# High and low weight parts for 24 units of layers 0 and 1, made at fixed places of ScalarE's and VectorE's programs

## The reference

```
# layer 0
h = rmsnorm(x); u_val, u_gate, z_a, q_b, k_b, v_b, z_b = split(h @ e_w_in)
y_a = conformer_conv(u_val, u_gate) * silu(z_a)
y_b = moba_attention(norm(q_b), norm(k_b), v_b) * silu(z_b)
x = x + concat(y_a, y_b) @ w_out[0]
# layer 1
h = rmsnorm(x); q_c, kc, vc, ks, vs, kw, vw, g_c, z_c, q_d, k_d, v_d, z_d = split(h @ o_w_in)
y_c = nsa_attention(...) * silu(z_c);  y_d = banded_attention(...) * silu(z_d)
x = x + concat(y_c, y_d) @ w_out[1]
# layer 2: modulated norm, retention and dilated attention, gates, then a squared-relu MLP
mod = silu(c) @ w_ada + b_ada          # 12 column groups, ad0 to ad11, spread over layers 0 and 1
x = x + g1 * token_mixer(modulate(rms_norm(x), sh1, sc1))
x = x + g2 * mlp(modulate(rms_norm(x), sh2, sc2));  out = rms_norm(x)
```

## Time and profile before

| | us |
|---|---|
| median of 3 runs | 1032.57 (1030.12 to 1032.97) |
| the profiled execution's own time | 1030.22 |
| its span | 1028.4 |
| PE busy | 957.8 (93%) |
| DVE, ACT, POOL busy | 363.5, 408.1, 446.0 |

### The profile page before, as it was taken

One profiled execution on the slowest core, in us unless ns is written; L12 is line 12 of the kernel. 1 busy time (PEld: TensorE's weight loads), 2 busy tenths in 40 slices (PEclk: granted clock), 3 DMA queues, 4 the chain that ended last, 5 costly groups with the idle time before them and its releaser, 6 DMA issues.

```text
span 1028.4 us, 15967 instructions
## 1 busy us (share of the span) xinstructions
PE 957.8 (93%) x6896; PEld 874.2 (85%) x6896; DVE 363.5 (35%) x734; ACT 408.1 (40%) x588; POOL 446.0 (43%) x101
## 2 busy tenths in 40 slices
PE   4999889999898798999999998999999979999996
PEld 4887677788676377999999998999999979999996
DVE  4677521320556626640111113222115643341002
ACT  3111541013576423234343444667533545553330
POOL 0000000000000031787766665766787767886780
PEclk9999899999899999999999998999999989999998
DMA  9632245858524363565534443444544625453531
GB/s 353 257 123 82 83 175 205 329 176 316 196 83 164 124 246 126 175 242 183 185 131 158 158 150 111 160 161 152 177 164 164 238 95 200 168 199 130 204 121 41
DMA packets 27470, 177.51 MB, mean 173 GB/s; under 512 B 2904, under 2 KB 5476, under 8 KB 6920
## 3 DMA queue, kind: packets, MB, share of 16 engines
q1 hardware_dynamic: 25960, 174.28, 46.9%
q10 hardware_dynamic: 1440, 2.20, 0.7%
HBM read 174.88 MB, written 3.43 MB: 173 GB/s over the span
## 4 chain that ended last, share of the span: by engine, by line
PE 84%; DVE 10%; ACT 3%; issue 1%; DMA 1%; POOL 0%; DVEq 0%; ACTq 0%
PE proj L571 18%; PE proj L596 14%; PE proj L597 14%; PE proj L598 14%; PE proj L628 3%; PE proj L630 3%; PE proj L629 3%; PE proj L780 3%; PE proj L617 2%; PE transposed L702 2%; PE proj L810 2%; PE mixed L731 1%; PE scores L690 1%; DVE parts L1561 1%; PE scores L677 1%
## 5 line engine op out<-in xcount | busy, mean ns | idle before, releaser
L521 POOL TENSOR_TENSOR w_lo<-raw,w_hi 128x2048 fp32r<-128x2048 f32 x71 | 329.0, 4639 | 269.7 <-ACT w_hi L1050 269.6
L596 PE MATMUL proj<-parts,w_hi 128*128 128x256 f32 x768 | 222.2, 289 | 6.5 <-DVE parts L1383 4.2
L597 PE MATMUL proj<-parts,w_lo 128*128 128x256 f32 x800 | 227.5, 284 | 0.0
L598 PE MATMUL proj<-parts,w_hi 128*128 128x256 f32 x768 | 218.3, 284 | 0.0
L1050 ACT ACTIVATE w_hi<-raw 128x2048 fp32r<-128x2048 f32 x71 | 135.5, 1909 | 99.4 <-PE proj L598 63.8
L596 PEld LDWEIGHTS proj<-parts,w_hi 128*128 128x128 f32 x768 | 148.1, 193 | 8.1 <-issue 5.2
L597 PEld LDWEIGHTS proj<-parts,w_lo 128*128 128x128 f32 x800 | 154.2, 193 | 0.8 <-issue 0.7
L598 PEld LDWEIGHTS proj<-parts,w_hi 128*128 128x128 f32 x768 | 148.0, 193 | 0.0
L525 POOL MEMSET probT<- 128x512 f32 x1 | 0.5, 525 | 247.8 <-PE proj L897 247.8
L571 PE MATMUL proj<-h,raw 128*128 128x256 f32 x320 | 76.5, 403 | 3.0 <-DVE h L1391 3.0
L571 PEld LDWEIGHTS proj<-h,raw 128*128 128x128 f32 x320 | 64.7, 204 | 14.2 <-issue 4.5
(11 more groups left out here) (273 smaller groups left out, 1940.5 us busy)
## 6 DMA issues: line engine op xcount, KB each, us to landing
raw<-in_weights SPq DMA_DIRECT2D x113, 1024.0 KB, 4.9
arena<-in_weights SPq DMA_DIRECT2D x36, 1024.0 KB, 5.0
probT<-in_weights SPq DMA_DIRECT2D x8, 1024.0 KB, 5.7
dil_lines<-dil_line SPq DMA_DIRECT2D x1, 2304.0 KB, 12.1
dil_bias<-dil_lines SPq DMA_DIRECT2D x1, 1536.0 KB, 9.6
xT<-in_x SPq DMA_DIRECT2D x2, 512.0 KB, 5.6
arena<-in_alibi SPq DMA_DIRECT2D x1, 1024.0 KB, 20.6
arena<-in_swa SPq DMA_DIRECT2D x1, 1024.0 KB, 7.3
```

The lines of the kernel that those rows point to most:

```text
L521: nc.gpsimd.tensor_tensor(lo_slots[RAW_AT[n]][:, 0:kt * w], raw_slots[RAW_AT[n]][:, 0:kt * w], hi_slots[HI_AT[m]][:, 0:kt * w].bitcast(F32 ...
L596: nc.tensor.matmul(dst, whi, h, start=first, stop=False)
L597: nc.tensor.matmul(dst, wlo, h, start=False, stop=False)
L598: last = nc.tensor.matmul(dst, whi, lo[:, k, :], start=False, stop=stop)
```

## The change

24 units of layers 0 and 1 (all that are not uv, ug, bq, bk, bv, kcvc, the ad units or the hidden layers' ck and cv) join the list `SPLIT`, and are multiplied as high and low parts, three products for one float32 matmul. For the first 23 of them ACT makes the high copy (`high`) and DVE, not POOL, the subtraction (`low`), each called at a place written into its program; the 24th, wo1_3, stays with POOL, which now begins its list with it. The activations are split too: h of layers 0 and 1 (`high_parts` without a shift), and the gated outputs yT0 and yT1. The raw slots and the order of the loads change: slots 6 to 8 hold parts too, slot 8 lies under h of layer 0 (`h0`) and is not used before bv1 is done, ad units from ad6 on use slots 0 to 3, and wo1_0 to wo1_2 are loaded ahead of ad7. The diff, cut to its core:

```diff
@@ tables @@
+    "/ zd1.1", "/ E:zd1 ad6", "/ modA", "/ ad7", "/ ad8", "Y:c / ad9", "/", "/ ad11")]
-SPLIT = WEIGHTS[WEIGHT_AT["rq0"]:]
+WHOLE = ("uv0", "ug0", "uv1", "ug1", "bq0", "bq1", "bk0", "bk1", "bv0", "bv1", "kcvc")
+SPLIT = [u for u in WEIGHTS if u not in WHOLE and u[:2] not in ("ad", "ck", "cv")]
+BY_POOL = SPLIT_AT["wo1_3"]
+HIGH_B, LOW_B = {1: "za1", 2: "wo0_0", 3: "wo0_1"}, {2: "za1", 3: "wo0_0"}
+HIGH_CD = {0: "zc1", 2: "zd0", 3: "zd1", 5: "wo1_0", 7: "wo1_1", 9: "wo1_2"}
+LOW_CD = {1: "zc1", 3: "zd0", 4: "zd1", 6: "wo1_0", 8: "wo1_1", 10: "wo1_2"}
@@ PE, weight(u) @@
-                pe.wait_ge(lo_ready, m + 1)
+                if m < BY_POOL:
+                    pe.wait_ge(sem("lo_early"), m + 1)
+                else:
+                    pe.wait_ge(lo_ready, m - BY_POOL + 1)
@@ PE, layer 1 @@
             project("kcvc", fresh=1)
+            pe.wait_ge(h_ready, 2 * KD)
             project("kskw")
-            plain_tokens("vsvw", 2 * P)
+            tokens("vsvw", 0, 2 * P)
...
-            plain_tokens("vdgt", P + 24)
+            tokens("vdgt", 0, P + 24)
@@ ACT @@
+            def high(u):
+                n, m = WEIGHT_AT[u], SPLIT_AT[u]
+                kt, w = unit_shape(u)
+                if HI_BEFORE[m] is not None:
+                    act.wait_ge(proj_ready, LAST_READ[SPLIT[HI_BEFORE[m]]] + 1)
+                act.wait_ge(raw_in[RAW_AT[n]], raw_target(n))
+                nc.scalar.activation(hi_slots[HI_AT[m]][:, 0:kt * w], raw_slots[RAW_AT[n]][:, 0:kt * w], ACT.Copy).then_inc(hi_ready, 1)
@@ ACT, output_squares: between the squares of one group and of the next @@
+                    if i < len(also):
+                        high(also[i])
-            output_squares(0, "x1")
+            output_squares(0, "x1", ("wo0_3", "kskw", "vsvw"))
+            high_parts("x1")
+            high("qc0")
@@ ACT, layer 1 @@
             root("kskw")
+            high("vdgt")
             head_squares("qc0", fl(qcT[:, 0:2]))
+            high("qd0")
             head_squares("qc1", fl(qcT[:, 2:4]))
+            high("zc0")
             root("qc0")
...
             hidden_copy(0, "hidk")
+            high("qd1")
             head_squares("qd0", fl(qdT[:, 0:2]))
+            high("kd")
             hidden_silu(0, "hTk", "c_k_b1")
@@ DVE @@
+            def low(u):
+                dve.wait_ge(hi_ready, m + 1)
+                V.tensor_tensor(lo_slots[RAW_AT[n]][:, 0:kt * w], raw_slots[RAW_AT[n]][:, 0:kt * w],
+                                hi_slots[HI_AT[m]][:, 0:kt * w].bitcast(F32), ALU.subtract).then_inc(sem("lo_early"), 1)
@@ DVE, layer 1 @@
             head_norm_end("kskw", "kskw", None, None)
-            for i, name in enumerate(("qc0", "qc1")):
+            low("qc1")
+            low("vdgt")
+            for name, unit in (("qc0", "qd0"), ("qc1", "zc0")):
+                low(unit)
                 variance(name)
                 head_norm_end(name, name, None, None)
+            low("qd1")
+            low("kd")
             variance("qd0")
```

More of the change, by code:

```diff
@@ L142, in raw_slots_of @@
 def raw_slots_of(n, u):
-    if u in SPLIT_AT:
+    if u[:4] == "ad10" or u[:3] == "wo1":
+        return EARLY
+    if u[:2] == "ad" and n > WEIGHT_AT["zd1"]:
+        return range(NRAW)
+    if n >= WEIGHT_AT["rq0"]:
         return range(NRAW + sum(n >= WEIGHT_AT[start] for start in RAW_MORE))
-    return EARLY if n >= WEIGHT_AT["wo1_0"] else [*range(NRAW), *EARLY]
+    return [*range(NRAW), *EARLY[:3 if n >= WEIGHT_AT["wo0_0"] else 2]]
 RAW_AT, RAW_BEFORE = take_slots(WEIGHTS, raw_slots_of)
@@ L156 @@
 LOADS.insert(LOADS.index("rq1") + 1, "wo1_3")
+for _n in range(3):
+    LOADS.remove(f"wo1_{_n}")
+    LOADS.insert(LOADS.index("ad7a"), f"wo1_{_n}")
 def loads_after():
@@ L1140, in between @@
                 if "." in name:
+                    return
+                if name[:2] == "Y:":
+                    operand_high([(hi_of(i), two(yT1, i), [(po_free, STEPS_TO["c"])]) for i in range(2)])
                     return
@@ L1187, in attention @@
                     transposed_out(u, range(1, key_tiles(u)))
+                    for made in (HIGH_B if UNITS[u][0] == "b" else HIGH_CD if UNITS[u][0] in "cd" else {}).get(i, "").split():
+                        high(made)
                     if UNITS[u][0] == "a":
@@ L1223, in _ @@
             root("bk0")
+            high("zb0")
             root("bk1")
+            high("zb1")
             copy_tokens("bv0", bv[:, :, 0:256])
+            high("za0")
             copy_tokens("bv1", bv[:, :, 256:512])
@@ L1228, in _, with output_squares @@
             attention(PART["b"], FILL_B)
+            operand_high([(hi_of(i), two(yT0, i), [(sem("y_a_ready"), i + 1)] if i < 2 else
+                           [(po_free, 2 * i - 2)]) for i in range(4)])
+            high("wo0_2")
             table(ACT.Sqrt)
-            def output_squares(layer, stream):
+            def output_squares(layer, stream, also=()):
                 for i in range(4):
@@ L1247, in _ @@
             head_squares("kskw", arena[:, L + 2048:L + 2560])
+            high("qc1")
             values = cut(ready("vsvw")[:], S)
@@ L1285, in _ @@
             attention(PART["c"] + PART["d"], FILL_CD)
+            operand_high([(hi_of(i), two(yT1, i), [(po_free, STEPS_TO["c"] + 2 * i - 2)]) for i in range(2, 4)])
             table(ACT.Sqrt)
@@ L1649, in conv_between @@
                         mixed_out(u - 1)
+                    if i in LOW_B:
+                        low(LOW_B[i])
                     if i == 0:
@@ L1675, in _ @@
             V.tensor_copy(bn[:, 1, 9:10], yT0[:, 0, 0:1]).then_inc(sem("conv_done"), 1)
+            for u in ("zb0", "zb1", "za0"):
+                low(u)
             conv_between(PART["b"])
+            parts_low(yT0)
+            low("wo0_1")
             def fold_squares(name, i):
@@ L1690, in residual @@
                     fold_squares(f"x{layer + 1}", i)
-            residual(0)
+                    if i < len(also):
+                        low(also[i])
+            residual(0, ("wo0_2", "wo0_3", "kskw"))
+            ada_out("ad2")
             stream_norm("x1", col("norm_g", 8, 8))
-            for name in ("ad2", "ad3"):
-                ada_out(name)
+            low("vsvw")
+            ada_out("ad3")
+            low("qc0")
             own.did(V.memset(blocks[:, :, :, 2 * NCMP:HROW], 0.0))
@@ L1724, in _ @@
             attention(PART["c"] + PART["d"], FILL_CD)
+            parts_low(yT1, range(2, 4))
             residual(1)
```

135 lines of the change are left out of this document (81 added, 54 removed).

## The result

The changed kernel takes **1072.37 us**, median of 4 runs (1069.89 to 1074.20); the kernel before took 1032.26 beside it (1030.12 to 1032.97, 4 runs). The ratio is 1.0391, with a 95% interval of 1.0362 to 1.0419. The profiled execution took 1073.51 with a span of 1071.7 (before 1030.22 and 1028.4), so the two spans, 43.3 apart, can be compared stage by stage.

What follows compares the result with a forecast made beforehand. PE, busy 93% of the span, was taken to bound the kernel. A gain of 20.5 us against added waits, vdgt and clock summed to +42.6 on 1032.6, so 1075 us; range 1057 to 1092, with rivals 2 to 5 1055 to 1095.

Steps and rivals of the forecast that it cites:

- The gain on PE: 18 full-width units outside the attention of layer 1, each 1.14 us shorter when split: -20.5 us.
- vdgt: Unit with 152 moving columns, taken to go no faster split than in float32, 12.7 us against 4.24: +8.5 us.
- Layer 0: Attention and output start of layer 0: PE waits 2.8 us for za1 and 3.8 at wo0_0 behind DVE's subtractions: +6.6.
- Squares of x1: End of layer 0: ACT's squares of wo0_3 stand behind vsvw's copy, which waits for its load: +7.9 us.
- qc1: Layer 1: DVE subtracts qc1 only behind the norm of kskw, so PE waits: +3.5 us.
- zc0 and qd1: Layer 1: ACT's copies wait for loads ahead of hidk's copy and qd0's squares; 6.0 and 11.1 us: +17.1 together.
- Attention of layer 1: Six copies and six subtractions delay PE's transposes by 13 us, less 3 from shorter half units: +10 us.
- Output of layer 1: wo1_3 stays with POOL, whose work meets the fold of squares, as before: net +0.5 us on top of the gain.
- Clock: Six waits of 2.8 to 8 us lower PE's granted clock behind them, 1.5 us each: +9 us.
- signs that were named: x1 sums wait over 6 us, copies wait 5 or more, vdgt 12, clock near 0.5; refuted if PE idles under 10.
- Rival 1: All new waits are covered and only PE's gain is left: 1007 to 1015 us; chance 0.05.
- Rival 5: POOL's later subtractions meet DVE's norm of x2, two collisions of 4.5 us: 1084 us; chance 0.05.

Runs made afterwards that it cites:

- e3: Changed kernel with DVE's subtractions of za1, wo0_0 and qc1 put earlier and ACT's copy of wo0_1 behind the high parts of yT0: 1065.38 us, ratio 1.0300.
- e6: The best version: e5 with ACT's high copy of zc0 behind the activation of hTk and the copy of hidv: 1017.63 us, ratio 0.9856.
- e5: Changed kernel with the moves of e1b, e2, e3 and the second reordering of layer 1's attention together: 1018.77 us, ratio 0.9862.
- e1: Changed kernel with ACT's copies and DVE's subtractions of zc0, qd1 and kd moved later in their programs: 1059.99 us, ratio 1.0258.
- e1b: e1 with the copies of qd1 and kd ahead of cmp's root, their subtractions ahead of cmp's variance: 1057.49 us, ratio 1.0238.
- e2: Changed kernel with ACT's copies of kskw and vsvw behind x1's squares and root, and DVE's subtraction of kskw later: 1062.27 us, ratio 1.0277.
- e7: e6 with ACT's squares ahead of its high copies for POOL's units in the output of layer 1: 1021.16 us, ratio 0.9895.

## Why the prediction was right, and where it was wrong

1075 was forecast and 1072.4 measured, on the mechanism that was named. By its steps:

- **The gain on PE** (-20.5): a split unit takes 5.8 us. PE's busy time in the best version is 934.7 us against 957.8, 23.1 less; 20.5, some 5 for the half units in the attention, and 1.1 back for vdgt make 24.6. The Trainium skill (FP8 and Floating Point Precision, TensorE Precision Notes) says that true FP32 makes four passes; by that the term would have been -31.1 without the half units, an estimate, and it is not seen.
- **vdgt** (+8.5): wrong. The step took the float32 row of the same shape as the nearer bound. Groups of the kernel after, 242.5 to 248.1 us:

```profile
L653 PE MATMUL proj<-w_hi,parts 128*128 128x152 f32 x16 | 4.4, 277 | 0.0
L654 PE MATMUL proj<-w_lo_e,parts 128*128 128x152 f32 x16 | 4.4, 276 | 0.0
L655 PE MATMUL proj<-w_hi,parts 128*128 128x152 f32 x16 | 4.4, 276 | 0.0
```

  The durations overlap; the 48 run from 242.61 to 248.0 at a clock of 1.00, 5.3 us against 4.24: +1.1. Neither bound held; it lies between them, nearer the low one.
- **Layer 0** (+6.6): the waits of 2.8 and 3.4 us are there. e3 gave 3.5 us of them back in this stage.
- **Squares of x1** (+7.9): the wait at the last sums is 5.7 us. kskw's copy had held the squares before, for which PE waits 1.8 us more, a wait that the forecast took for nothing. Together they are 7.5. Moving both copies gave 11.3 us in the stage (98.3 to 86.9), its clock included.
- **qc1** (+3.5): the wait is 3.5.
- **zc0 and qd1** (+17.1): waits of 5.9, 7.4 and 1.4 where 6.0 and 11.1 were forecast; with their clock the move gave 16.9 us in the stage.
- **Attention of layer 1** (+10): the stage grew by 15.0. PE's busy time in it is 3.5 us above that of the best version, with the same instructions: clock, which the forecast had as a term of its own. That leaves some 11.5 for the term.
- **Output of layer 1** (-4.6 of gain, +0.5): -2.4 measured. The step that failed is "PE waited before too": ACT's squares of wo1_1 now stand 3.4 us behind the load of wo1_3, POOL's wo1_3 begins beside the fold of wo1_1, and PE waits 2.8 us at the sums where it was 1.9. Behind that wait the granted clock is 0.72 (430 to 436 us), so that PE's busy time in the stage fell by only 3.3 us (32.4 to 29.1) and not by 4.6.
- **Clock** (+9): mis-sized. The kernel after and e6 have the same 7272 matmuls; PE is busy 951.7 us in the one and 934.7 in the other, 17 us apart, of which 4.1 lie in layer 0, 8.1 in layer 1, 3.5 in its attention. e6 may stand for the kernel before here: its mean granted clock is 0.973 and that one's 0.976, against 0.951 in the kernel after. The 17 us are nearly a third of what the moves gave back, beside waits that add up to about 32 us outside the attention. The forecast had taken 1.5 a wait from one row; in layer 1 a wait of 1.6 us alone cost 3.4 in e5, and about half of that in e1 and e1b.

Of the signs that were named, ACT's four copies waited 7.9 to 12.1 us for their loads (5 or more), PE was idle 14.5 us from 195 to 262 us (10 or more), and the clock was 0.50 behind the waits at the sums of x1, at hTk and at the sums of qd0. Two did not come: the wait at the sums of x1 was 5.7 and not over 6, and vdgt took 5.3 us and not 12.

So vdgt (7.4 too high) and the clock (8 too low) nearly cancel; the sum is closer than its terms, and that is luck. Rival 1 was rightly small for this order of the programs. Its reason, that no timing of ACT changes when a slot is freed, was too strong: the slot's time is fixed, but what stands behind the copy isn't, and e2 and e1 made most of the cost vanish without an earlier load. Rival 5 (POOL falls behind) did not come in the changed kernel, and in e7 only in part, with one collision in the norm of x2 (3.16 us for 1.28) where it had two of 4.5.

## What to carry to other kernels

An engine with a fixed program and 40% of load is not free: before putting an instruction into it, look at what it will wait for and at what stands behind it there, and put it after the work that is due and before the engine's own next wait. A copy from a slot that the running group still holds belongs behind everything that this group's end releases. When a change adds work to helpers and comes out slower, read which releasers the waits name: if they name old work, reorder before giving the change up.

## What was not expected of the hardware

A split matmul with 152 moving columns takes 0.111 us (5.3 over 48) and one with 256 takes 0.120: 41% fewer columns save 7%. A float32 matmul takes 0.265 and 0.432, so there the columns count nearly in proportion (0.61 for 0.59), and splitting, which pays 1.14 us on a unit of 256, loses 1.1 on one of 152. And one wait of 1.6 us among small matmuls was followed by a clock of 0.50 for nearly 7 us in e5 and for some 3.3 in e1 and e1b, where one of 1.55 us between ad4 and zc0 left it at 1.00 (e6).
